# Two transformer blocks in one kernel: turns of normed and plain query tiles, a shorter refinement of roots, and clearing on GpSimd in the projection

## The reference

```python
h = modulate(rms_norm(x, norm1_g[l]), sh1, sc1)
hc = modulate(rms_norm(xc, norm1_g[l]), csh1, csc1)
qa, ka, va, qb, kb, vb, ga, gb = split_in_proj(h @ w_in[l])
qac, kac, vac, qbc, kbc, vbc, gac, gbc = split_in_proj(hc @ w_in[l])
qb = rms_norm(qb, q_norm_g[l])
kb = rms_norm(kb, k_norm_g[l])
kbc = rms_norm(kbc, k_norm_g[l])
ya = window_attention_latent(apply_rope(qa, cos, sin), apply_rope(ka, cos, sin), va, kac, vac, sink_a[l])
yb = full_attention_latent(apply_rope(qb, cos, sin), apply_rope(kb, cos, sin), vb, kbc, vbc)
```

## Time and profile before

| | |
|---|---|
| median of 3 runs | 2652.49 us (2652.48 to 2653.84) |
| the profiled execution | 2660.09 us, span 2658.3 us |
| PE busy | 2426.4 us, 91% of the span |
| DVE busy | 1562.9 us, 59% |
| ACT busy | 1105.5 us, 42% |
| POOL busy | 132.3 us, 5% |

### The profile page before, as it was taken

How to read it: one execution, slowest core, us unless ns; L and a number is a source line. 1 busy time by engine, 2 the same in 40 slices (tenths; PEclk the granted TensorE clock), 3 DMA queues, 4 the chain that set the end, 5 groups by cost and what they waited for, 6 DMA issues and landing times.

```text
span 2658.3 us, 32137 instructions
## 1 busy us (share of the span) xinstructions
PE 2426.4 (91%) x12095; PEld 2008.4 (76%) x12095; DVE 1562.9 (59%) x2383; ACT 1105.5 (42%) x1752; POOL 132.3 (5%) x243
## 2 busy tenths in 40 slices
PE   6978888889799999999797999889999989988898
PEld 2767777778678888888675777678888867867687
DVE  2664657678855555553675677653333367377763
ACT  2435656752332122122444677343222255456451
POOL 0000000011000000000000000100000000000010
PEclk9999989999899999999898999999999989989999
DMA  5211011145343333332221111423222224512153
GB/s 222 104 43 47 35 36 42 42 173 211 111 160 128 118 135 127 118 111 72 96 79 44 48 48 48 170 74 101 96 95 95 94 93 143 170 65 65 67 190 111
DMA packets 67744, 267.68 MB, mean 101 GB/s; under 512 B 8416, under 2 KB 8480, under 8 KB 66448
## 3 DMA queue, kind: packets, MB, share of 16 engines
q1 hardware_dynamic: 41616, 154.16, 16.9%
q0 software_dynamic: 25984, 111.55, 11.7%
HBM read 237.37 MB, written 27.26 MB: 100 GB/s over the span
## 4 chain that ended last, share of the span: by engine, by line
PE 77%; DVE 9%; ACT 7%; issue 6%; DMA 1%; POOL 0%; POOLq 0%; ACTq 0%; DVEq 0%
PE ps L183 21%; PE ps L184 21%; PE ps L185 21%; PE ps L969 1%; PE ps L971 1%; PE ps L970 1%; ACT pr L1024 1%; ACT hf L419 1%; PE ps L953 1%; PE ps L488 1%; DVE wt_out L313 1%; PE ps L910 1%; PE ps L917 1%; DVE maxes L1105 1%; DVE w_lo L179 1%
## 5 line engine op out<-in xcount | busy, mean ns | idle before, releaser
L183 PE MATMUL ps<-h_hi,w_hi 128*128 128x512 f32 (+1 forms) x2328 | 874.0, 375 | 89.9 <-DVE spread L1141 25.6
L184 PE MATMUL ps<-h_lo,w_hi 128*128 128x512 f32 (+1 forms) x2328 | 857.9, 368 | 0.0
L185 PE MATMUL ps<-h_hi,w_lo 128*128 128x512 f32 (+1 forms) x2328 | 856.7, 368 | 0.0
L183 PEld LDWEIGHTS ps<-h_hi,w_hi 128*128 128x128 f32 x2328 | 450.3, 193 | 178.2 <-issue 68.6
L184 PEld LDWEIGHTS ps<-h_lo,w_hi 128*128 128x128 f32 x2328 | 450.6, 194 | 74.0 <-issue 2.1
L185 PEld LDWEIGHTS ps<-h_hi,w_lo 128*128 128x128 f32 x2328 | 448.8, 193 | 76.4
L179 DVE TENSOR_TENSOR w_lo<-w_raw,w_hi 128x1024 fp32r<-128x1024 f32 x288 | 351.4, 1222 | 256.3 <-ACT w_hi L172 255.9
L172 ACT ACTIVATE w_hi<-w_raw 128x1024 fp32r<-128x1024 f32 x288 | 302.9, 1053 | 336.5 <-PE ps L185 312.4
L185 PE MATMUL ps<-q_hi,w_lo 128*128 128x512 f32 x720 | 257.0, 357 | 0.0
L184 PE MATMUL ps<-q_lo,w_hi 128*128 128x512 f32 x720 | 256.7, 357 | 0.0
L183 PE MATMUL ps<-q_hi,w_hi 128*128 128x512 f32 x720 | 256.3, 356 | 0.0
(11 more groups left out here) (331 smaller groups left out, 2933.8 us busy)
## 6 DMA issues: line engine op xcount, KB each, us to landing
w_raw<-in_stream SPq DMA_DIRECT2D x288, 512.0 KB, 3.3
wt<-in_ada_t POOLq DMA_DIRECT2D x80, 512.0 KB, 3.6
ada_raw<-in_ada POOLq DMA_DIRECT2D x4, 2048.0 KB, 15.2
x_keep<-x POOLq DMA_DIRECT2D x8, 768.0 KB, 5.7
gates<-th_g POOLq DMA_DIRECT2D x16, 384.0 KB, 2.6
x<-x_keep POOLq DMA_DIRECT2D x2, 3072.0 KB, 12.8
gates<-sg POOLq DMA_DIRECT2D x24, 256.0 KB, 2.3
gates<-th_g POOLq DMA_DIRECT2D x16, 256.0 KB, 2.3
```

Of the source, the lines that this page charges most:

```text
L183: nc.tensor.matmul(out_ap, lh, rh, start=start, stop=False)
L184: nc.tensor.matmul(out_ap, lh, rl, start=False, stop=False)
L185: return nc.tensor.matmul(out_ap, ll, rh, start=False, stop=stop)
```

## The change

There are three edits.

- **Order of queries.** `Q_ORDER` = (4, 0, 5, 1, 6, 2, 7, 3) sets the order of the query tiles in `layer_tiles` and, with it, that of the weight units in the packed stream. A normed tile and a plain one now come in turn, and the last one is plain.
- **Refinement.** In the projections `newton` is called with `scaled=True` and takes three operations: y becomes (s - 3 width) x y, which is the refined root times -2 width. ScalarE's copy of a normed tile gets the factor -0.5 / 64 in addition, which makes up for it. The other calls keep four operations.
- **Clearing.** GpSimd does it, behind the same wait as before on the norm. Each memset waits for the one in front of it. In a stacked projection there are ten of them, then the copies of `x`; in the second block two, which count five each.

```diff
--- before.py
+++ after.py
@@ -30,6 +30,7 @@
 LRU_C = 8.0
 W_LEN = 912
 UNIT = 1024
+Q_ORDER = (4, 0, 5, 1, 6, 2, 7, 3)
 
 
 N_QKV, N_GATE, N_MERGE, N_OUT = 12, 16, 8, 8
@@ -450,10 +451,13 @@
                         if c == CH - 1:
                             mm.then_inc(unit_done, 1)
 
-        def newton(e, sums, y, width, done=None):
+        def newton(e, sums, y, width, done=None, scaled=False):
 
             dve_own.link(e, nc.vector.scalar_tensor_tensor(sums, sums, width * EPS, y, ALU.add, ALU.mult))
             dve_own.link(e, nc.vector.tensor_tensor(sums, sums, y, ALU.mult))
+            if scaled:
+                dve_own.link(e, nc.vector.scalar_tensor_tensor(y, sums, -3.0 * width, y, ALU.add, ALU.mult))
+                return
             dve_own.link(e, nc.vector.tensor_scalar(sums, sums, -0.5 / width, 1.5, ALU.mult, ALU.add))
             last = nc.vector.tensor_tensor(y, y, sums, ALU.mult)
             if done:
@@ -569,6 +573,7 @@
             q_home = qf if stacked else r_q1["qf2"]
             width = [t[2] for t in tiles]
             normed = [t[3] is not None for t in tiles]
+            factor = [t[5] * (1.0 if t[3] is None else -0.5 / HD) if t[0] != "raw" else None for t in tiles]
             T = len(kinds)
             before = lambda flags: np.cumsum([0] + [int(f) for f in flags]).tolist()
             n_sq = before(normed)
@@ -684,7 +689,7 @@
                         e.wait_ge(stat.sem, stat.base + n_st[t - 1])
                     elif t >= 2 and k != "Q":
                         e.wait_ge(low.sem, low.base + n_hl[t - 1])
-                    nc.scalar.activation(home(t)[:, 0:w], src, ACT.Copy, scale=tiles[t][5]).then_inc(copied.sem, 1)
+                    nc.scalar.activation(home(t)[:, 0:w], src, ACT.Copy, scale=factor[t]).then_inc(copied.sem, 1)
                     if normed[t]:
                         if n_qk[t] >= 2:
                             e.wait_ge(shaped.sem, shaped.base + n_qk[t] - 1)
@@ -716,16 +721,6 @@
                 if opening:
                     e.wait_ge(tables_loaded, 48)
                     nc.vector.tensor_copy(band[:, :], r_q2["pr"][:, 0, 0:3 * P]).then_inc(table_done, 1)
-                for j in range(2):
-                    if stacked:
-                        dve_own.link(e, nc.vector.memset(k_lo[64:128, 2 * j, :].bitcast(F32), 0.0))
-                        dve_own.link(e, nc.vector.memset(k_lo[0:64, 2 * j + 1, :].bitcast(F32), 0.0))
-                        nc.vector.memset(k_lo[64:65, 2 * j, :].bitcast(F32), 1.0).then_inc(zeroed.sem, 2)
-                        nc.vector.memset(k_lo[0:1, 2 * j + 1, :].bitcast(F32), 1.0).then_inc(zeroed.sem, 2)
-                    else:
-                        e.sem_inc(zeroed.sem, 4)
-                nc.vector.memset(v_hi[:, :, :, 64:128].bitcast(F32), between).then_inc(zeroed.sem, 1)
-                nc.vector.memset(v_lo[:, :, :, 64:128].bitcast(F32), 0.0).then_inc(zeroed.sem, 1)
                 if not stacked:
                     e.wait_ge(y_kept, 1)
                 for t in range(T + 2):
@@ -771,7 +766,7 @@
                 e.wait_ge(copied.sem, copied.base + t + 1)
                 if normed[t]:
                     e.wait_ge(rough.sem, rough.base + n_sq[t + 1])
-                    newton(e, psf[:, at(t):at(t) + w], y[:, 0:w], HD)
+                    newton(e, psf[:, at(t):at(t) + w], y[:, 0:w], HD, scaled=True)
                     ins = nc.vector.scalar_tensor_tensor(z[:, 0:w], z[:, 0:w], tiles[t][3], y[:, 0:w], ALU.mult, ALU.mult)
                     if tiles[t][4]:
                         dve_own.link(e, ins)
@@ -788,8 +783,16 @@
                 nc.vector.tensor_tensor(z[:, 0:SEQ], z[:, 0:SEQ], spin, ALU.add).then_inc(shaped.sem, 1)
 
             def pool(e):
+                e.wait_ge(norm.low.sem, norm.low.base + CH)
+                parts = [(v_hi[:, :, :, 64:128], between), (v_lo[:, :, :, 64:128], 0.0)]
                 if stacked:
-                    e.wait_ge(norm.low.sem, norm.low.base + CH)
+                    parts += [(k_lo[dn, 0, :], 0.0), (k_lo[dn, 2, :], 0.0), (k_lo[up, 1, :], 0.0), (k_lo[up, 3, :], 0.0),
+                              (k_lo[64:65, 0, :], 1.0), (k_lo[64:65, 2, :], 1.0), (k_lo[0:1, 1, :], 1.0), (k_lo[0:1, 3, :], 1.0)]
+                each = 10 // len(parts)
+                for n, (part, value) in enumerate(parts):
+                    nc.gpsimd.memset(part.bitcast(F32), value).then_inc(zeroed.sem, each)
+                    e.wait_ge(zeroed.sem, zeroed.base + each * (n + 1))
+                if stacked:
                     for j in range(4):
                         e.dma_start(x_keep[:, 2 * j:2 * j + 2, :], x[:, 2 * j:2 * j + 2, :]).then_inc(spilled.sem, 16)
                     return
@@ -817,7 +820,7 @@
             w = TOK if both else SEQ
             kg, qg, sc = col("kg", layer), col("qg", layer), HD ** -0.5
             return [("K", 0, TOK, None, True, 1.0), ("v", 0, TOK, None, False, 1.0), ("K", 1, TOK, kg, True, 1.0),
-                    ("v", 1, TOK, None, False, 1.0)] + [("Q", j, w, qg if j >= 4 else None, True, sc) for j in range(8)]
+                    ("v", 1, TOK, None, False, 1.0)] + [("Q", j, w, qg if j >= 4 else None, True, sc) for j in Q_ORDER]
 
 
         def attention_and_gates(layer, both):
@@ -2384,9 +2387,8 @@
     w = a["w_in"][l]
     for at in (512, 640, 1280, 1408):
         yield unit_of(w[:, at:at + P])
-    for at in (0, 768):
-        for j in range(PAIRS):
-            yield unit_of(w[:, [at + r for r in PAIR[j]]])
+    for j in Q_ORDER:
+        yield unit_of(w[:, [768 * (j // PAIRS) + r for r in PAIR[j % PAIRS]]])
     for n in range(16):
         yield unit_of(w[:, 1536 + P * n:1536 + P * n + P])
     rows = sum(PAIR, [])
```

## The result

The changed kernel took 2620.64 us (median of 4, 2618.40 to 2623.92), the kernel before 2653.16 us beside it. The ratio is 0.9872, 95% interval 0.9858 to 0.9887. The forecast was 2629.3 with a range from 2622: the direction held, and the gain of 32.5 us is 9 us more than the 23.2 forecast. The profiled execution took 2621.99 us, span 2620.2.

A forecast was written before the change was run, and what follows sets the result against it. TensorE work was taken as the bound (77% of the span), so only its waits in the first two projections could pay. Gains of 11.1 and 12.1 us, 23.2 in all, took the median of 2652.5 to 2629.3 us, range 2622 to 2642.

The forecast's parts named there:

- the chain: Layer 0's projection: 5.6 us from the front, 5.5 from the tail; layer 1's projection 12.1 us, its front 6.2 us earlier.
- another engine's gap: Clearing on GpSimd: self-wait of about 0.25 us taken from VectorE's chained pair, giving 0.98 us per memset.
- the sum: Projections of layers 0 and 1: 11.1 + 12.1 = 23.2 us gained, nothing from the second block.

The follow-up runs named there:

- the changed kernel's second and third: The changed kernel run again without alteration, each time against the kernel before: 2618.7 us (ratio 0.9856), then 2621.7 us (0.9885).

## What to carry to other kernels

Where TensorE waits, work that others could do beside it belongs on an idle engine and the tile with the shortest finish belongs last; both paid here what the chain said. Price a chained operation by a pair on its own engine, since another engine's gap may differ fourfold (here 0.22 and 0.06 us). And a wait of TensorE can cost more than its length: in this kernel 2.2 us more of it in each of two places cost 13.5 us by the medians (with some 7 us of scatter either way), and twice that pause cost hardly more, 14.8. So shortening one may return more than the sum says, in stretches that the change never touched, and the range should be open on that side.

## What the hardware showed that I had not expected

- A cast on VectorE suffered beside GpSimd's memset, though two-input operations did not. The first row is the kernel before, the second the changed one, where it lies beside the first memset. It took 0.98 us in all thirteen profiles with the clearing on GpSimd (the changed kernel's second and third too) and 0.36 in the five others; the second memset, which starts during it, took 0.83 us, and 0.74 in layer 1, where there is no cast.

```profile
77.24 0.36 DVE L718 CAST band<-pr 128x384 fp32r<-128x384 f32 x1
```

```profile
76.54 0.98 DVE L723 CAST band<-pr 128x384 fp32r<-128x384 f32 x1
```

- One program, unchanged, differs from one execution to the next in single stretches, and by fixed steps. Two profiles of the changed program, the one of its third set of runs first, weight units 22 to 26: 87.59 us at clock 1.00 against 91.07 at 0.93, with the same 423 matmuls. In all eighteen profiles, whatever the kernel, these units took either 87.5 to 87.6 us or 91.0 to 91.1.

```profile
362.72:450.31 87.59, 77.07 (x423) 65.79 (x424) 58.91 (x86) 59.69 (x108) 2.17 (x4) 1.00 0.12 43
```

```profile
363.30:454.37 91.07, 82.40 (x423) 70.20 (x424) 59.08 (x86) 59.76 (x109) 2.17 (x4) 0.93 0.12 41
```

- Two versions have to be compared by several executions each: single ones of the kernel before ran from 2648.9 to 2663.6 us, the one of 3986 us aside.
